# Second block's attention: the queries' sums of squares by transposes and a VectorE reduction in place of products with a column of ones

## What is computed

```
q = (rms_norm(c_q, q_norm_g) @ w_uq).reshape(B, S, 8, 96)
kv = (rms_norm(c_kv, kv_norm_g) @ w_ukv).reshape(B, S, 8, 64 + 64)
k_nope, v = kv[..., :64], kv[..., 64:]
k = concatenate([k_nope, broadcast(k_rope)], axis=-1)
q = rms_norm(q, qk_q_g)          # per token and head, over the 96 features
k = rms_norm(k, qk_k_g)
q = concatenate([q[..., :64], apply_rope(q[..., 64:], cos, sin)], axis=-1)
k = ...                          # the same
out = softmax(q @ k.T * 96 ** -0.5, causal) @ v
```

## Time and profile before

| | us |
|---|---|
| Median of 3 runs | 3573.86 |
| The runs | 3572.23, 3575.67, 3573.86 |
| The profiled execution | 3573.54 |
| Its span, first to last instruction | 3571.7 |
| Busy: PE, DVE, ACT, POOL | 3499.8, 2024.9, 1232.3, 1419.7 |

### The profile page before, as it was taken

The page is one execution under the profiler, slowest core; times in us unless marked ns, Lnnn a source line. Parts: engine busy times, 40 slices in busy tenths (PEclk is TensorE's granted clock), DMA queues, the critical chain, the costliest instruction groups (busy, mean ns, idle before and its releaser), DMA issues.

```text
span 3571.7 us, 42483 instructions
## 1 busy us (share of the span) xinstructions
PE 3499.8 (98%) x15976; PEld 2716.5 (76%) x15976; DVE 2024.9 (57%) x2581; ACT 1232.3 (35%) x2133; POOL 1419.7 (40%) x754
## 2 busy tenths in 40 slices
PE   8999999999999999999999999999999999999999
PEld 7888676788878888766788877877766778776667
DVE  6423666643267522666553356974756489466653
ACT  4443334202212443334301223133556221445542
POOL 3444222352266444322352356533422355342224
PEclk9999999999999999999999999999999999999999
DMA  4223111431143232201341133211111231111122
GB/s 165 100 106 118 61 30 30 159 118 37 43 142 128 90 117 106 75 27 36 116 156 36 36 124 111 97 42 36 48 30 34 80 125 48 36 49 35 33 68 95
DMA packets 88675, 278.73 MB, mean 78 GB/s; under 512 B 9648, under 2 KB 10672, under 8 KB 87984
## 3 DMA queue, kind: packets, MB, share of 16 engines
q1 hardware_dynamic: 48960, 159.08, 14.4%
q10 hardware_dynamic: 39536, 117.13, 8.9%
HBM read 220.59 MB, written 55.57 MB: 77 GB/s over the span
## 4 chain that ended last, share of the span: by engine, by line
PE 88%; DVE 7%; ACT 2%; issue 2%; POOL 1%; DMA 0%; SPq 0%; ACTq 0%; POOLq 0%; DVEq 0%
PE psA L531 30%; PE psT L512 17%; PE psA L512 9%; PE psA L903 7%; PE psT L903 7%; PE psA L2188 3%; PE psT L2259 2%; PE psT L2170 2%; PE psT L865 2%; PE psA L820 1%; PE psT L804 1%; DVE b_wk L1560 1%; PE psT L2236 1%; PE psT L2165 1%; DVE b_wk L2715 1%
## 5 line engine op out<-in xcount | busy, mean ns | idle before, releaser
L478 POOL TENSOR_TENSOR Whi<-stage,credit 128x1024 fp32r<-128x1024 f32 (+1 forms) x276 | 495.4, 1795 | 1809.0 <-PE psT L512 890.7
L481 POOL TENSOR_TENSOR Wlo<-stage,Whi 128x1024 fp32r<-128x1024 f32 (+1 forms) x276 | 670.5, 2429 | 21.7
L512 PE MATMUL psT<-Hhi,Whi 128*128 128x512 f32 x1024 | 424.4, 414 | 8.4 <-DVE b_wk L1548 3.2
L531 PE MATMUL psA<-Hhi,Whi 128*128 128x512 f32 x1312 | 414.3, 397 | 0.7 <-DVE b_ypad L2705 0.4
L531 PE MATMUL psA<-Hlo,Whi 128*128 128x512 f32 x1312 | 404.4, 389 | 0.0
L512 PE MATMUL psT<-Hhi,Wlo 128*128 128x512 f32 x1024 | 404.3, 395 | 0.0
L531 PE MATMUL psA<-Hhi,Wlo 128*128 128x512 f32 x1312 | 404.0, 389 | 0.0
L512 PE MATMUL psT<-Hlo,Whi 128*128 128x512 f32 x1024 | 403.6, 394 | 0.0
L531 PEld LDWEIGHTS psA<-Hhi,Whi 128*128 128x128 f32 x1312 | 244.8, 188 | 62.1 <-issue 12.1
L531 PEld LDWEIGHTS psA<-Hlo,Whi 128*128 128x128 f32 x1312 | 246.2, 188 | 51.8
L531 PEld LDWEIGHTS psA<-Hhi,Wlo 128*128 128x128 f32 x1312 | 246.2, 188 | 51.7
(11 more groups left out here) (389 smaller groups left out, 6723.5 us busy)
## 6 DMA issues: line engine op xcount, KB each, us to landing
stage<-in_w SPq DMA_DIRECT2D x264, 512.0 KB, 3.5
gs<-b_wk ACTq DMA_DIRECT2D x62, 512.0 KB, 2.7
b_wk<-gs ACTq DMA_DIRECT2D x46, 512.0 KB, 4.9
stage<-in_w SPq DMA_DIRECT2D x68, 256.0 KB, 2.7
xs<-X ACTq DMA_DIRECT2D x8, 2048.0 KB, 8.1
b_wk<-xs ACTq DMA_DIRECT2D x32, 256.0 KB, 4.3
rope<-gs ACTq DMA_DIRECT2D x14, 512.0 KB, 5.1
b_wk<-xs ACTq DMA_DIRECT2D x14, 512.0 KB, 4.3
```

What stands on the lines that cost most here:

```text
L478: pool.tensor_tensor(Whi[:, b, 0:n], stage[:, b, 0:n], credit[:, 0:1].broadcast_to([P, n]), ALU.add).then_inc(s.w_hi, 1)
L481: pool.tensor_tensor(Wlo[:, b, 0:n], stage[:, b, 0:n], Whi[:, b, 0:n].bitcast(F32), ALU.subtract).then_inc(s.w_split, 1)
L512: mm = pe.matmul(dst[0:M], w[:, cols], r[k][:, c], start=k == 0 and w is whi and r is rhi, stop=k == nk - 1 and end)
L531: mm = pe.matmul(dst[h], w[:, cols], r[k][:, h * HALF:(h + 1) * HALF], start=first and k == order[0] and r is rhi and w is whi, stop=last ...
```

## The change

TensorE turns the four blocks of 128 tokens of `QSQ` (96 rows) into four blocks of 96 columns of one bank, with the tokens on the partitions, in place of four products with one column of ones. VectorE adds the 96 columns of each block into four columns of `half_root`, and frees the bank. ScalarE waits for that, takes Ln in place in SBUF and Exp as before. On VectorE the piece stands right behind the division of its step (behind what was put off), is no longer put off, and is put into the list of the prelude twice; the prelude's third one follows the maxima of the first step.

```
-B2_HANDLED = [("q", 0, 0, 0), ("q", 0, 1, 0), ("vt", 0, 0, 0), ("ks", 0, 0, 0), ("q", 0, 0, 1), ("ks", 0, 1, 0),
-              ("vt", 0, 1, 0)]
+B2_HANDLED = [("q", 0, 0, 0), ("q", 0, 1, 0), ("st", 0, 0, 0), ("vt", 0, 0, 0), ("ks", 0, 0, 0), ("st", 0, 1, 0),
+              ("q", 0, 0, 1), ("ks", 0, 1, 0), ("vt", 0, 1, 0)]
...
                     for t in range(NT // 2):
-                        mm = pe.matmul(psF[:, t:t + 1], QSQ[sd][QK, t * P:(t + 1) * P], ones[QK, 0:1], start=True, stop=True)
+                        mm = pe.transpose(psF[:, t * M_QK:(t + 1) * M_QK], QSQ[sd][QK, t * P:(t + 1) * P], ident[QK, QK])
...
-                act.wait_ge(*F.filled(L, use))
+                act.wait_ge(*(F.drained(L, use) if kind == "st" else F.filled(L, use)))
...
-                    act.activation(r, psF[:, 0:NT // 2], ACT.Ln, bias=epsc[:, 0:1], scale=1.0 / M_QK)\
-                        .then_inc(F.freed(use), 1)
-                    act.wait_ge(*F.drained(L, use))
+                    root_step.step(act, act.activation(r, r, ACT.Ln, bias=epsc[:, 0:1], scale=1.0 / M_QK))
                     act.activation(q_root[:, p % 2, sd, blocks], r, ACT.Exp, bias=lnscale[:, 0:1], scale=-0.5)\
                         .then_inc(q_rs.sem, 1)
...
+                elif kind == "st":
+                    dve.wait_ge(*F.filled(L, use))
+                    if p:
+                        dve.wait_ge(*q_rs.upto(L, half_at(p - 1, sd, half) + 1))
+                    dve.reduce_sum(half_root[:, sd, half], psF[:, 0:NT // 2 * M_QK].rearrange("p (t c) -> p t c", c=M_QK),
+                                   AX_X).then_inc(F.freed(use), 1)
...
-                            if use[0] == "vt" or use in pair_pieces(p, i, 0) and use[0] == "o":
+                            if use[0] in ("st", "vt") or use in pair_pieces(p, i, 0) and use[0] == "o":
                                 piece(L, use)
```

## The result

The changed kernel takes 3581.26 us (median of 11 runs, 3578.28 to 3584.95), beside 3572.51 us for the kernel before, measured with it: a ratio of 1.0026, 95% interval 1.0017 to 1.0035. It is slower by about 9 us, a quarter of a per cent. The forecast was 3579 us, 5.7 us over the kernel before; by the interval it is 6 to 12.5 us. The profiled executions differ by 7.1 us of span (3578.8 and 3571.7).

The account below looks back on a forecast made before the run. TensorE was taken as the bound (busy 98% of the span, 88% of the chain). Preludes +2.4, step 15 -1.2, step 10 +1.8, step 5 +0.3 and step 2 +2.4 sum to +5.7 us on 3573.5: 3579 us, range 3564 to 3589.

Parts of the forecast that it names:

- the loop's terms: Pieces outside the preludes: step 15 -1.2 us, step 10 +1.8, step 5 +0.3, step 2 +2.4.
- preludes: Three pieces a layer: keys, low parts and first probabilities come later; +1.2 us a layer, +2.4 in all (0.6 to 4).
- TensorE's piece: Four transposes at 0.36 us replace products at 0.85 in each of 32 pieces: 0.49 us saved (0.33 to 0.61).
- reduction: VectorE's sum over 384 elements from PSUM, priced from its copies: 0.55 us a piece (0.42 to 0.69).
- Ln from SBUF: ScalarE's Ln reads SBUF instead of PSUM: taken as the same 0.26 us, ends 0 and +0.04.
- step 15: Six pieces: the bank is freed earlier for the following kv piece; -0.2 us each, -1.2 in all.
- step 10: Six pieces: maxima wait behind the reduction, TensorE's turns for VectorE's division; saving lost and 0.3 more each, +1.8 us (0 to 3.6).
- step 5: Six pieces: later Ln uses up ScalarE's idle time before the kv squares; saving gone, +0.3 us in all (-3 to +1).
- step 2: Eight pieces: Ln slips 0.9 to 1.2 us; five hidden, one costs 0.8, last pairs' two 0.85 each; +2.4 us (0.5 to 4).
- Rival 1: Saving stays at steps 5, 10, 15, preludes and first pairs, nothing lost elsewhere: 3562 us; chance 0.15.
- Rival 2: Gains and losses cancel: prelude costs 0.3 a layer, step 10 nothing, step 5 keeps half its saving: 3574 us; chance 0.18.
- Rival 3: At pair boundaries and one prelude TensorE falls to half clock: 7 us on top, 3586 us; chance 0.22.

Follow-up runs that it names:

- e1: The changed kernel without its reduction: TensorE transposes everywhere, ScalarE takes Ln straight from PSUM of one column in 96; 3561.97 us, ratio 0.9972 to the kernel before.
- e2: The changed kernel with the four products back and VectorE copying four sums where it reduced, ScalarE waiting for that copy; 3580.19 us, ratio 1.0025 to the kernel before.
- e4: Only the three st pieces of each prelude changed, the loops' 26 pieces as in the kernel before; 3580.22 us, ratio 1.0021 to the kernel before.
- e5: The changed kernel with each of its 32 reductions made twice on VectorE; 3596.20 us, ratio 1.0071 to the kernel before.
- e12: Kernel before with st pieces of steps 5, 10 and 15 changed, logarithm at step's end, step 10's reduction behind the next division; 3565.42 us, ratio 0.9988.
- e7: The changed kernel with ScalarE's logarithm and exponential of the loop's st pieces moved to the step's end; 3574.25 us, ratio 1.0010 to the kernel before.
- e3: The changed kernel with the three st pieces of each layer's prelude computed as before; 3572.05 us, ratio 1.0000 to the kernel before.
- e6: The changed kernel with ScalarE's logarithms and exponentials of the prelude's st pieces put later; 3580.13 us, ratio 1.0027 to the kernel before.
- e9: The changed kernel with VectorE's prelude reordered: five low parts before the second reduction, third reduction behind the first division; 3583.37 us, ratio 1.0030 to the kernel before.
- e11: Kernel before with only the 12 st pieces of steps 5 and 15 turned and reduced, ScalarE's logarithm at the step's end; 3565.89 us, ratio 0.9985.
- e10: The changed kernel with TensorE releasing GpSimd's mid-prelude weight split at the third q piece's last tile, not its first; 3578.72 us, ratio 1.0019 to the kernel before.

## Why the prediction was right, point by point

The time was in the range, 2 us from the number. The mechanism, a saving lost at the link, holds (e1, e2), and the loop's terms hold in sum: +3.3 forecast, +3.3 found. The preludes' term is 5.5 us too small. All places together come to 11.2 us, twice the 5.7 of the forecast; that the runs came out 8.75 us apart, near the forecast, is in part luck.

| term | forecast | aligned traces | what decides |
|---|---|---|---|
| TensorE's piece | -0.49 | e1: -0.54 at step 5, -0.52 at 10, -0.24 at 15, -0.06 at the last step 2; -0.22 a prelude | e1 |
| reduction | 0.55 us | 0.557 us | the line itself |
| Ln from SBUF | 0 to +0.04 | 0.30 for 0.26, +0.04 | the line itself |
| preludes | +2.4 | +7.9 (4.14 and 3.77) | e4: +7.6 |
| step 15 (6) | -1.2 | -1.2 (-0.19 each) | e1 -0.24, e2 0.00 |
| step 10 (6) | +1.8 | +0.8 (+0.13 each) | e5, e12 |
| step 5 (6) | +0.3 | +0.8 (four at -0.25, two at +0.91) | e7 |
| step 2 (8) | +2.4 | +2.9 (two at 0.82, four at 0.32, two at 0) | e7; e3 beside e4 |
| sum | +5.7 | +11.2 | the runs: +8.75 (6 to 12.5) |

The two profiled spans are only 7.1 us apart: the stretches from step 2 to 5 of the first three pairs are 2.6 us shorter in the changed kernel's trace although they cost 1.3, since the trace of the kernel before has more of TensorE's slow clock there (e4, above). The fourth piece of 0.32 us is in the second layer's third pair, where e6 and e9 have +0.32, and e7 and e11, without ScalarE's wait, 0.00. The runs put the loop at 0 within 3 us (e3) and the preludes at 7.6 (e4).

- **The prelude** is the term that failed. The step said that the keys start 1.7 us later (they did, by 1.6 with the offset of 0.25 between the traces), the low parts at 2532.2 and TensorE's q piece ends 1.6 us later. The low parts started at 2533.3, and TensorE waited 3.60 us. What was left out is GpSimd. The rows had it: the rotation at 2035 ns against 690 was seen, and taken as something that a later instruction might escape. A later one can also run into it. The five low parts were read as 0.96 us each, the mean of a merged row, where four take 0.67 and one, behind GpSimd, 2.37. In the kernel before they began 0.5 us ahead of the split, the split waited (3.70 us) and only the fifth was held; this margin was the thing to price.
- **Step 15** came out as forecast, -0.19 for -0.2 each. TensorE's saving alone is worth 0.24 there and the link nothing (e1, e2).
- **Step 10**: the saving is lost there as said, and by the wait named: the turns of step 11 wait for VectorE's division, though 0.13 us is paid on top and not 0.3. That the maxima behind the reduction are what counts is shown by e5 (+0.59 for 0.56 us more) and by e12, where the reduction stands behind the division.

```profile
2588.48 0.33 PE L2170 MATMUL psT<-ident,b_wk 128*128 128x128 f32 x1 [0.41 <-DVE b_wk L2854]
```

- **Step 5**: the price was averaged over pairs. Two pairs gain 0.25; in the third the rotation takes 1.85 us, beside GpSimd's low half of the split (2699.02 to 2701.39), and ScalarE's wait grows to that length.
- **Step 2** in the last pairs is as forecast (0.82 for 0.85), and by the cause given, ScalarE's queue: e7 takes it away. Of the others one was to cost 0.8 and five nothing; in fact four cost 0.32 each.
- **Rival 1** is the kernel e1, at 3562 us as worked out: what the change would be without its reduction (though step 15 gives half of the 0.5 us that it assumed). **Rival 2** describes the loop alone (e3). **Rival 3**, the clock: e1 has all 128 transposes and is the faster by 10 us, and the slow stretches moved in every execution, with old code too (e4). So it is not the price of the transposes, as that rival had it. Wholly out it is not. The changed kernel's eleven runs have a mean granted clock of 0.992, the 82 runs of the kernel before that were measured with the experiments 0.9936, and among these 82 the runs at 0.993 take 3572.9 us on average and those at 0.994 3569.8. By that some 3 of the 9 us go with the clock; whether it is lower because TensorE stops in the preludes, as before 2536, no run separates.

## What to carry to other kernels

A link that goes through a second engine is priced by that engine's queue at each place where it stands, and not by its own length alone: find what is queued behind the wait on both engines, and put the waiting instruction at the last point at which its result is needed. Where an operation is moved on VectorE by a microsecond, look at what GpSimd begins in that microsecond, and at which of VectorE's operations it will hold: in the first prelude five low parts took 4.8 us before and after, and TensorE stopped only where the first of them was the held one. If an edit is repeated at many places, price and test the places apart: 12 of the 32 pieces here made the kernel faster than both, while all 32 made it slower.

## What the runs showed of the hardware

- A VectorE operation on two operands in SBUF and a GpSimd split instruction exclude one another, and the held VectorE operation ends 0.55 us after the GpSimd instruction, whatever is left of its own length: the key operation at 2532.94 (split's first half to 2532.40), the first low part at 2535.69 (second half to 2535.14), the kernel before's fifth low part at 2534.72 (2534.17), and so, within 0.02 us, do all 122 operations of the preludes, over the 14 traces, that took more than 1 us. A low part that isn't held takes 0.67 to 0.68 us. So five of them take 3.08 us with none held (e10; the change's second layer), 4.76 to 4.78 with one held, 6.84 with two (e6). Who goes first isn't settled by the recorded starts. While the split waits, low parts that begin after its recorded start go past it: three in the kernel before, all five in the changed kernel's second layer, where the split took 5.08 us, against 1.89 to 1.93 where it hardly waited. That stays open. The row of the kernel before that belongs to the earlier trace rows, where the low parts were 0.5 us ahead and the split waited:

```profile
2530.48 3.70 POOL L478 TENSOR_TENSOR Whi<-stage,credit 128x1024 fp32r<-128x1024 f32 x1 [3.94 <-PE psT L512]
```

The Trainium skill says this of the port pair that the two engines share ("SBUF — State Buffer", the section on its two separate sides): whoever starts first holds it for the whole instruction and the other is blocked. The traces agree that the held one is blocked and does not share, with the numbers above; that the first to start has it they show for the held operations, and not for the low parts that go past a waiting split. The reduction and the copies, which read PSUM, kept their 0.54 to 0.56 and 0.41 us beside a split.

- What decided who came first in the changed kernel's second layer was TensorE's clock. The granted clock of 3207 to 3212 was 0.67 (windows, below), its passes took 0.63 us instead of 0.39 at 3209, the third q piece, whose first pass releases the split, began later, and the split at 3211.25 missed the keys. In e4, with the same prelude, the clock was 1.00 there, the split came 0.2 us ahead of the second key operation, and the prelude cost 4.97 us: a slower stretch of one engine made it 2.5 us shorter (1.1 to the third reciprocal).

```profile
3207.00:3212.00 5.00, 4.13 (x14) 3.35 (x15) 3.35 (x7) 2.61 (x6) 0.75 (x1) 0.67 0.33 105
```
- VectorE's copy of 4 columns out of PSUM takes 0.16 us, its sum over 384 columns 0.557.
